# Choosing the prompt's first experts head by head, in a fused two-layer diffusion step

## The chip, the cores and the metric

The kernel runs as one program on one core of a Trainium2 chip. The metric is the device time of one execution in microseconds (us); lower is better. The engines are called PE (TensorE, matmuls), DVE (VectorE), ACT (ScalarE), POOL (GpSimd) and SP (SyncE, which here only starts transfers).

## The reference, cut to what matters

Two layers run over a prompt block of 128 tokens and a sample of 256 tokens, called P and S. Layer 0 mixes with a bidirectional mLSTM, layer 1 with attention; behind each mixer comes a layer that picks, for each token and each of 8 heads, 16 of 16384 experts. That layer is what the change is about:

```python
def one_block(xb):                                     # 128 tokens
    q = (xb @ w_q).reshape(128, P_HEADS, 2, 128)
    s = jnp.einsum('tphd,phnd->tphn', q, subkeys)      # 128 keys in each of two sets a head
    s1, i1 = lax.top_k(s[:, :, 0], 16)
    s2, i2 = lax.top_k(s[:, :, 1], 16)
    cand = (s1[..., :, None] + s2[..., None, :]).reshape(128, P_HEADS, 256)
    cidx = (i1[..., :, None] * 128 + i2[..., None, :]).reshape(128, P_HEADS, 256)
    top, pos = lax.top_k(cand, 16)
    eidx = jnp.take_along_axis(cidx, pos, axis=-1)
    g = jax.nn.softmax(top, axis=-1)
    act = gelu(jnp.einsum('tped,td->tpe', u[eidx], xb))
    return jnp.einsum('tpe,tped->td', g * act, v[eidx])
```

The prompt's mLSTM also returns its final state (`new_C`, `new_n`, `new_m`, each for two directions).

## The kernel before, in words

**Six phases of gathers.** Each pair of a layer and a token block (three blocks, two layers) is a phase of 64 groups of two expert slots. For every slot POOL starts one indirect transfer, which brings for each of 128 tokens its expert's row of u and v (8 KB): 1 MB a slot, 768 slots in all. DVE forms the dot product with u against `xrep`, the tokens copied for it; ACT makes gelu, the share and a small diagonal matrix; PE adds v times that matrix into `acc`. The rows live in a ring of 14 places (`rows`, 7 groups). From the second turn on POOL waits until the group that had the place before is summed.

**One order for all engines.** `plan()` writes the whole program as a list of steps, and each engine walks it in order (`in_order` moves a few steps on ACT and DVE). Steps named here: `NT` puts the normalised tokens transposed into `hT`; `PQ` is a quarter of the query projection (4 PSUM tiles, copied out by ACT), `PS` the scores of that quarter's two heads; `PT` the top 16 of each key set, `PC` the candidates' top 16, `PG` the experts' numbers, `PW` the shares; `MLU` is the state update of one direction (four PSUM tiles, copied out by DVE), `STATE` starts the state's transfers to memory on ACT's queue; `XR` makes `xrep` (4 PSUM tiles a half, copied by ACT); `MR` and `MC` compute a part of the modulation; `GROUPS` are groups of experts. There are six PSUM tiles, used in turn: PE can open the next only when the engine that empties it has read what stood there six tiles before.

**Where weights are put.** SP walks a list of loads of 512 KB (`weight_loads`). Before the first gathers the expert rows are free, so the first 99 loads take turns over 33 places: five of `wt` and 28 halves of `rows`. From the load after `("MR", 1, 0, 3)` on only the five places of `wt` are used. A load waits until the PSUM tile that last used its place is full (`sp.wait_ge(tile_full, free)`), and SP starts its loads in order. POOL's first 14 gathers wait in the same way for the last use of their row as a weight place.

**The opening of the first phase.** The prompt's first quarter of the choice was split in two heads already, but with one projection and one score tile. The steps stand as NT, MLU twice, STATE, PQ 0, PS 0, PQ 1, XR twice; then come the choices of head 0 and head 1. The scores and candidates lie in `sc` and `cand`, which share their memory with what the state's transfers read, so `PC` of head 0 waits for those:

```python
if s[1:] == (*FIRST_SCORES[1:], 0):

    dve.wait_ge(state_out, 96)
```

POOL's first gather waits for the first increment of `experts_chosen`, which is the end of head 0's `PG`.

Of the kernel before, what the change touches and what calls it, by code (L numbers as in the profile page):

```python
# [19 lines left out]
P = 128  # L20
# [66 lines left out]
def plan():  # L87
# [157 lines left out]
FIRST_SCORES = ("PS", 0, "P", 0, 0)  # L245
# [5 lines left out]
def in_order(who):  # L251
# [27 lines left out]
def psum_tiles(s):  # L279
# [29 lines left out]
    if k == "PQ":  # L309
        return "AAAA"  # L310
# [17 lines left out]
def weight_tiles(s, A):  # L328
# [19 lines left out]
    if k == "PQ":  # L348
        return cols(A["peer_w_q"], 8 * s[1] + 2 * s[3], 2, 2)
    if k == "PS":  # L350
        return [(A["subkeys"][QUARTERS * s[1] + s[4]], nb_of(s) - 1)]
# [3 lines left out]
EARLY = WRING + 2 * RING * GS  # L355

def weight_loads(A):
# [29 lines left out]
def needed(i, who):  # L388
# [6 lines left out]

    if s[0] in ("PT", "PC", "PG", "PW") and s[1:5] == FIRST_SCORES[1:]:
        return PLAN.index(FIRST_SCORES) + 1
# [8 lines left out]
    if s[0] == "XR":  # L406
        return after("NT") if who == "P" else PLAN.index(FIRST_SCORES)
# [47 lines left out]
def trunk(nc, A, O):  # L455
    ctx = ExitStack()
    with ctx:
# [338 lines left out]
        def _(pe):  # L796
# [48 lines left out]
            def by_feature(n_tokens):  # L845

                for j in range(2):
# [77 lines left out]
            for n_entry in in_order("P"):  # L925
# [121 lines left out]
                elif k == "PQ":  # L1047
                    by_feature(P * len(BLOCKS[s[2]]))
# [65 lines left out]
        def _(act):  # L1114
# [54 lines left out]
            for n_entry in in_order("A"):  # L1169
# [143 lines left out]
                elif k == "PQ":  # L1313
                    _, l, g, q = s
                    n = P * len(BLOCKS[g])
                    for i in range(4):
                        copy_tile(i, qTp[:, 4 * q + i, 0:n], n)
# [68 lines left out]
        def _(dve):  # L1386
# [46 lines left out]

            def weigh(s):

                _, l, g, b, part, *half = s
                blk = BLOCKS[g][b]
                nh = 1 if half else QH
                part = half[0] if half else part
                n = slice(part * nh * TOPK, (part + 1) * nh * TOPK)  # L1440
                gs, gr = (gsum[:, 2 * part:2 * part + 2], grec[:, part:part + 1]) if half else (gsum, grec)
                dve.wait_ge(top_exp, next_of(top_exp))
                V.reciprocal(gr[:, 0:nh], gs[:, nh:2 * nh]).then_inc(dve_chain, one())
                dve.wait_ge(dve_chain, noted())
                shares = topc[:, part * nh:(part + 1) * nh, :].rearrange("p c (j k) -> p k c j", k=2)
                gates = gate[:, blk, n].rearrange("p (j c t) -> p t c j", c=nh, t=2)
                for h, t, kk in QUADRANT_MOVES:
                    src, dst = quadrant(2 * h + t), quadrant(2 * h + kk)
                    last = V.tensor_tensor(gates[dst, t], shares[src, kk], bc(gr[src, 0:nh], TOPK // 2), ALU.mult)  # L1449
# [5 lines left out]
            for n_entry in in_order("D"):  # L1455
# [14 lines left out]
                if k == "GROUPS":  # L1470
                    if s[3] == 0:

                        dve.wait_ge(experts_chosen, QUARTERS * GORDER.index((s[1], s[2])) + 1 + (s[1:3] != (0, 0)))
# [199 lines left out]
                elif k == "OUT":  # L1673
# [18 lines left out]
                    last.then_inc(dve_step, 1)  # L1692
                elif k == "PS":
                    n = slice(2 * QH * s[4], 2 * QH * (s[4] + 1))
                    if s[3] == 0:
# [3 lines left out]
                elif k == "PT":  # L1699
# [3 lines left out]
                    if len(s) > 5:  # L1703
                        n = slice(2 * s[5], 2 * s[5] + 2)
                        scores = scores[:, n, :]
                    top16(top1[:, n, :], i1u[:, n, :], [scores[:, e, :] for e in range(n.stop - n.start)])
                elif k == "PC":
# [5 lines left out]
                    if s[1:] == (*FIRST_SCORES[1:], 0):  # L1713

                        dve.wait_ge(state_out, 96)
                    at = 0
                    for i0, m, w in PAIRS:
                        c4 = cand[:, 0:nh, at:at + m * w].rearrange("p h (i j) -> p h i j", j=w)
# [4 lines left out]
                    top16(topc[:, n, :], posu[:, n, :], [cand[:, h, 0:NPAIRS] for h in range(nh)])  # L1723
                elif k == "PW":
                    weigh(s)
                elif k == "PG":
# [23 lines left out]
                    place_of = [cand[:, 0:nh, :].rearrange("p a b -> p (a b)"), sc[:, 2 * part * nh:2 * (part + 1) * nh, :].rearrange("p a b -> p (a b)")]  # L1750
# [26 lines left out]
                    dve.wait_ge(dve_chain, noted())  # L1777
                    chosen = [e12[:, a, n].rearrange("p (c j k) -> p k c j", c=nh, k=2) for a in range(2)]
# [5 lines left out]
                    if not half:  # L1784
                        weigh(s)
# [161 lines left out]
```

## Time and profile before

| what | value |
|---|---|
| three timed runs | 2361.65, 2361.05, 2360.09 us; median 2361.05 |
| the profiled execution, its own time | 2359.27 us |
| its span in the profile | 2357.5 us |
| busy, share of the span | PE 67%, DVE 66%, POOL 37%, ACT 36% |
| moved | 956.48 MB, mean 406 GB/s |
| mean granted clock of PE | 0.814 |

The span runs from the first to the last instruction; the execution's own time has 1.77 us more around it. Busy shares are means over stages with different limits, so no engine's share says by itself what the kernel waits for.
### The profile page before, as it was taken

What the parts mean: (1) busy time and instruction counts of PE and PEld (TensorE: products, weight loads), DVE (VectorE), ACT (ScalarE), POOL (GpSimd) and SP (SyncE); (2) the same over time, 40 slices, a digit from 0 to 9 for tenths busy, and PEclk for the clock granted to TensorE, in tenths of its full rate; (3) what the DMA queues carried; (4) which work ended last, traced back from release to release, by engine and by line L of the source; (5) the groups of instructions that cost most, each with busy time, mean ns of one, the idle gap of its engine ahead of it and who ended that gap; (6) DMA issues with size and microseconds to landing.
All of it is one profiled execution on the core that took longest, in us unless ns stands there. A gap on an engine that the chain in (4) does not pass through costs nothing. (4 is left out here: it accounts for less than half of the span.)

```text
span 2357.5 us, 29053 instructions
## 1 busy us (share of the span) xinstructions
PE 1569.6 (67%) x9366; PEld 845.2 (36%) x9366; DVE 1567.3 (66%) x4321; ACT 844.8 (36%) x2753; POOL 867.2 (37%) x772
## 2 busy tenths in 40 slices
PE   8897977787846556556646676788766545555554
PEld 6784734565521112324321353455433102100010
DVE  2357988557677795465796567665765897665654
ACT  2324355423222333453233435443322334232232
POOL 0014334433424325243435343424434444444351
PEclk8998988898976667878967898888889777777777
DMA  9979999999999999999999999999999999999996
GB/s 387 408 269 414 373 397 415 417 418 415 416 418 420 419 419 420 417 371 419 417 420 421 418 404 420 414 381 401 418 419 420 422 420 421 422 422 421 422 422 273
DMA packets 156955, 956.48 MB, mean 406 GB/s; under 512 B 19076, under 2 KB 21764, under 8 KB 58500
## 3 DMA queue, kind: packets, MB, share of 16 engines
q0 software_dynamic: 110592, 805.36, 82.5%
q1 hardware_dynamic: 40880, 144.94, 15.6%
q10 hardware_dynamic: 5332, 4.33, 0.7%
q8 instruction: 75, 1.23, 0.2%
q14 instruction: 76, 0.62, 0.1%
HBM read 951.67 MB, written 2.89 MB: 405 GB/s over the span
## 5 line engine op out<-in xcount | busy, mean ns | idle before, releaser
L789 POOL DMA_INDIRECT rows<-in_uv,eidx x768 | 866.9, 1129 | 1449.3 <-PE acc L872 1067.1
L1429 DVE CUSTOM_DVE_ANT_0 rows<-rows,xrep 128x1024 f32<-128x1024 f32 x768 | 911.9, 1224 | 380.0 <-DMA rows<-in_uv,eidx 354.5
L872 PE MATMUL acc<-rows,diag 128*32 128x512 f32 x3072 | 745.6, 747 | 494.4 <-ACT diag L1119 463.5
L872 PEld LDWEIGHTS acc<-rows,diag 128*32 128x32 f32 x3072 | 151.9, 126 | 978.2 <-ACT diag L1119 628.8
L1119 ACT ACTIVATE act_out<-act_in 128x2 f32<-128x2 f32 x384 | 77.6, 202 | 944.4 <-DVE act_in L1429 898.4
L807 PE MATMUL bank<-wt,hT 128*128 128x256 f32 x888 | 204.0, 389 | 23.9 <-DMA wt<-in_attn_w_qkv 6.9
L1119 ACT ACT_TABLE_LOAD x123 | 157.8, 1283 | 166.4 <-DVE act_in L1429 74.3
L1119 ACT ACTIVATE diag<-small,wv 128x32 f32<-128x32 f32 x768 | 204.9, 314 | 12.5
L807 PEld LDWEIGHTS bank<-wt,hT 128*128 128x128 f32 x888 | 170.5, 194 | 62.9 <-issue 18.7
L1119 ACT ACTIVATE wv<-act_out,gate 128x1 f32<-128x1 f32 x768 | 184.3, 287 | 12.6
L807 PE MATMUL bank<-hT,wt 128*128 128x256 f32 (+1 forms) x896 | 175.0, 356 | 9.8 <-DMA wt<-in_peer_w_q 6.5
L807 PEld LDWEIGHTS bank<-hT,wt 128*128 128x128 f32 x896 | 152.5, 194 | 39.1 <-issue 9.9
L834 PE MATMUL bank<-small,arena 128*128 128x128 f32 x216 | 41.2, 352 | 103.4 <-DVE arena L1499 38.8
L1119 ACT ACTIVATE arena<-bank 128x256 f32<-128x256 f32 (+2 forms) x150 | 50.3, 376 | 164.3 <-PE bank L807 136.1
L807 PE MATMUL bank<-small,hT 128*32 128x128 f32 (+1 forms) x1584 | 75.8, 309 | 16.9 <-issue 12.5
L834 PEld LDWEIGHTS bank<-small,arena 128*128 128x128 f32 x216 | 33.5, 184 | 120.1 <-issue 115.5
L807 PEld LDWEIGHTS bank<-small,hT 128*32 128x32 f32 (+1 forms) x1584 | 62.6, 128 | 32.0 <-issue 25.1
L1429 DVE DVE_READ_ACCUMULATOR2_ANT act_in<- 128x1 f32 x768 | 63.8, 83 | 0.0
L807 PE MATMUL bank<-wt,cs 128*32 128x256 f32 x480 | 49.4, 451 | 11.1 <-DMA wt<-in_ada_w 11.0
L807 PE MATMUL bank<-arena 128*128 128x257 f32 (+3 forms) x232 | 50.9, 432 | 6.0 <-DVE arena L1647 4.4
L1686 DVE TENSOR_TENSOR arena<-bank,Nn 128x256 f32<-128x256 f32 x24 | 10.2, 424 | 66.6 <-PE bank L807 66.6
L834 PE MATMUL bank<-small,hT 128*128 128x128 f32 x112 | 24.3, 393 | 45.1 <-ACT hT L1119 35.9
(177 smaller groups left out, 1446.0 us busy)
## 6 DMA issues: line engine op xcount, KB each, us to landing
wt<-in_ada_w SPq DMA_DIRECT2D x60, 512.0 KB
wt<-in_peer_w_q SPq DMA_DIRECT2D x48, 512.0 KB
rows<-in_ada_w SPq DMA_DIRECT2D x36, 512.0 KB, 15.0
wt<-in_mlstm_w_in SPq DMA_DIRECT2D x27, 512.0 KB
rows<-in_uv,eidx POOLq DMA_INDIRECT x768
wt<-in_attn_w_qkv SPq DMA_DIRECT2D x24, 512.0 KB
rows<-in_mlstm_w_in SPq DMA_DIRECT2D x21, 512.0 KB, 15.9
rows<-in_peer_w_q SPq DMA_DIRECT2D x16, 512.0 KB, 13.7
```

The costliest lines, as they stand in the source:

```text
L789: nc.gpsimd.indirect_dma_start(out=rows[:, r, :], out_offset=None, in_=A["uv"], in_offset=bass.IndirectOffsetOnAxis(ap=eidx[:, b, slot:slo ...
L807: return nc.tensor.matmul(out, lhsT, rhs, start=start, stop=stop)
L834: last = nc.tensor.transpose(out[:, i * P:(i + 1) * P], a, ident)
L872: last = nc.tensor.matmul(acc[c:c + QUAD, h * 512:(h + 1) * 512], diag[:, r, :], rows[:, r, D + h * 512:D + (h + 1) * 512], start=first, s ...
L1119: return nc.scalar.activation(out, in_, func, **kw)
L1429: last = V.tensor_tensor_reduce(out=rows[:, r, 0:D], in0=rows[:, r, 0:D], in1=xrep[:, GS * odd + j, :], scale=1.0, scalar=0.0, op0=ALU.mul ...
L1686: V.tensor_tensor(tmp, t[:, 0:WC], gbc[:, c], ALU.mult).then_inc(dve_freed, 1)
```

## The change

Six things are changed together, all in the opening of the first phase.

1. `PQ 0` and `PS 0` are cut by heads: a projection of two PSUM tiles, then the scores of that head alone (two matmuls over 128 tokens), for head 0 and then head 1.
2. The scores of these two heads go to blocks 1 and 2 of `eidx` and their candidates to blocks 1 and 2 of `gate`, tables which the sample needs only later. The wait for the state's transfers is gone.
3. `MLU` (twice) and `STATE` stand behind `PQ 1`, and on DVE head 1's choice stands behind the copies of `MLU`.
4. The experts are dealt to slots by four quadrants of tokens, 16 moves of 32x4 in place of 8 of 32x8 for each head; POOL may begin group 0 after head 0's first 8 moves and group 1 after all 16.
5. Groups of the first 16 take the halves of `xrep` in turn (`upper`, `starts`), not the first eight the lower and the next eight the upper one.
6. The 33 early weight places are used in another order (`LAP`), which starts with `rows`.

```diff
-    yield from (("NT", 0, 1, 0), *cell(["MLU"], 0), *cell(["MLU"], 1), ("STATE",))
-    yield from (("PQ", 0, "P", 0), ("PS", 0, "P", 0, 0), ("PQ", 0, "P", 1), ("XR", 0, 0, 0), ("XR", 0, 0, 1))
-    yield from ((k, 0, "P", 0, 0, half) for half in range(2) for k in ("PT", "PC", "PG"))
-    yield from (("PW", 0, "P", 0, 0, half) for half in range(2))
+    yield ("NT", 0, 1, 0)
+    for head in range(2):
+        yield from (("PQ", 0, "P", 0, head), ("PS", 0, "P", 0, 0, head))
+    yield from (("PQ", 0, "P", 1), *cell(["MLU"], 0), *cell(["MLU"], 1), ("STATE",), ("XR", 0, 0, 0), ("XR", 0, 0, 1))
+    for head in range(2):
+        yield from ((k, 0, "P", 0, 0, head) for k in ("PT", "PC", "PG"))
+    yield ("PW", 0, "P", 0, 0)
...
-FIRST_SCORES = ("PS", 0, "P", 0, 0)
+FIRST_SCORES = [("PS", 0, "P", 0, 0, head) for head in range(2)]
...
-        for k, half in (("PW", 1), ("PW", 0), *((k, half) for half in (1, 0) for k in ("PG", "PC", "PT"))):
-            i = PLAN.index((k, *FIRST_SCORES[1:], half))
-            order.remove(i)
-            order.insert(order.index(PLAN.index(FIRST_SCORES)) + 1, i)
+        for behind, steps in ((FIRST_SCORES[0], [(k, *FIRST_SCORES[0][1:]) for k in ("PT", "PC", "PG")]),
+                              (("MLU", "P", 1, 0), [*((k, *FIRST_SCORES[1][1:]) for k in ("PT", "PC", "PG")), ("PW", 0, "P", 0, 0)])):
+            for s in reversed(steps):
+                i = PLAN.index(s)
+                order.remove(i)
+                order.insert(order.index(PLAN.index(behind)) + 1, i)
...
+LAP = [*range(WRING, WRING + 20), *range(WRING), *range(WRING + 20, EARLY)]
...
-                place = n % EARLY if i <= last_early else n % WRING
+                place = LAP[n % EARLY] if i <= last_early else n % WRING
...
+        first_sc = eidx[:, 1:3, :].bitcast(F32)
+        first_cand = gate[:, 1:3, :].rearrange("p a b -> p (a b)").unsqueeze(1)
...
-            return (0, QG // 2) if order == 0 else (0, 1)
+            return 0, 1
...
-            return g // (QG // 2) if (order, g // QG) == (0, 0) else g % 2
+            return g % 2
...
-                    if g % QG == 0 or g == QG // 2:
-                        pool.wait_ge(experts_chosen, g // QG + 1 + (g > 0))
+                    if g % QG == 0 or g in (1, QG // 2):
+                        pool.wait_ge(experts_chosen, g // QG + 1 + (g > 0) + (g > 1))
...
+                elif s in FIRST_SCORES:
+                    if s == FIRST_SCORES[0]:
+                        _, place, turn, _ = loads[used[0]]
+                        used[0] += 1
+                        first_keys = weight_place(place)
+                        pe.wait_ge(w_in[place], 16 * turn)
+                    t = open_tile(0)
+                    for a in range(2):
+                        e = 2 * s[5] + a
+                        last = mm(t[:, a * NKEYS:(a + 1) * NKEYS], qTp[:, e, 0:P], first_keys[:, e * NKEYS:(e + 1) * NKEYS], True, True)
+                    last.then_inc(tile_full, 1)
...
+                elif s in FIRST_SCORES:
+                    dve.wait_ge(tile_full, full(0))
+                    V.tensor_copy(first_sc, tile(0)[:, 0:2 * NKEYS].rearrange("p (e n) -> p e n", n=NKEYS)).then_inc(dve_freed, 1)
...
-                    if s[1:] == (*FIRST_SCORES[1:], 0):
-
-                        dve.wait_ge(state_out, 96)
+                    pairs = first_cand if len(s) > 5 else cand
...
+                    if half:
+                        chosen = [e12[:, a, n].rearrange("p (j k) -> p k j", k=QUADS) for a in range(2)]
+                        experts = eidx[:, blk, n].rearrange("p (j q) -> p q j", q=QUADS)
+                        for q in range(QUADS):
+                            for kk in range(QUADS):
+                                last = V.scalar_tensor_tensor(experts[quadrant(kk), q], chosen[0][quadrant(q), kk], 1.0 / PACK,
+                                                              chosen[1][quadrant(q), kk], ALU.mult, ALU.add)
+                            if q == QUADS - 1 or (q == 1 and half == [0]):
+                                last.then_inc(experts_chosen, 1)
+                        continue
```

The instructions of PE from the transposes of `NT` to the projection `PQ 3`, before. `arena,xrep` with 257 columns is `MLU`, `hT,rows` or `hT,wt` a projection (`x32` is a whole quarter), `rows,arena` the scores, and `small,hT` with 32 rows is `XR`.

```order
L834 MATMUL bank<-small,arena 128x128 x8
L807 MATMUL bank<-arena,xrep 128x257 x8
L807 MATMUL bank<-hT,rows 128x128 x32
L807 MATMUL bank<-rows,arena 64x128 x8
L807 MATMUL bank<-hT,rows 128x128 x32
L807 MATMUL bank<-small,hT 32x128 x128
L807 MATMUL bank<-rows,arena 64x128 x8
L807 MATMUL bank<-hT,rows 128x128 x32
L807 MATMUL bank<-rows,arena 64x128 x8
L807 MATMUL bank<-hT,rows 128x128 x32
```

The same stretch of PE in the changed kernel:

```order
L848 MATMUL bank<-small,arena 128x128 x8
L821 MATMUL bank<-hT,rows 128x128 x16
L821 MATMUL bank<-rows,arena 128x128 x2
L821 MATMUL bank<-hT,rows 128x128 x16
L821 MATMUL bank<-rows,arena 128x128 x2
L821 MATMUL bank<-hT,rows 128x128 x32
L821 MATMUL bank<-arena,xrep 128x257 x8
L821 MATMUL bank<-small,hT 32x128 x128
L821 MATMUL bank<-rows,arena 64x128 x8
L821 MATMUL bank<-hT,rows 128x128 x32
L821 MATMUL bank<-wt,arena 64x128 x8
L821 MATMUL bank<-hT,wt 128x128 x32
```

`MLU` has moved from ahead of the first projection to behind the third piece of it, directly ahead of `XR`; head 0's scores stand behind 16 matmuls in place of 40.

The instructions of DVE between the second half of `NT` (`hT`) and the choice of head 0, before:

```order
L1507 TENSOR_SCALAR hT<-bank,gain,modT 128x128 x4
L1655 COPY arena<-bank 128x257 x8
L1698 COPY arena<-bank 128x512
L1406 MAX Nn<-arena 128x8 x2
L1409 MAX_INDEX arena<-Nn,arena 128x8 x2
L1412 MATCH_REPLACE arena<-Nn,arena 128x128 x2
L1415 MAX Nn<-arena 128x8 x2
L1418 MAX_INDEX arena<-Nn,arena 128x8 x2
```

In the changed kernel the copies of `MLU` (128x257) stand here, between head 0's last step and head 1's first:

```order
L1811 SCALAR_TENSOR_TENSOR arena<-arena 128x16
L1814 TENSOR_TENSOR eidx<-eidx,Nn 128x256
L1816 TENSOR_REDUCE arena<-eidx 128x16
L1823 SCALAR_TENSOR_TENSOR eidx<-arena 32x4 x16
L1730 COPY eidx<-bank 128x256
L1690 COPY arena<-bank 128x257 x8
L1432 MAX Nn<-eidx 128x8 x2
```

The eight copies no longer stand between `NT` and head 0; the copy that empties head 1's score tile stands behind all of head 0's moves.

The loads that SP starts around the first phase's opening, before (the last row's first four loads use the `wt` places that `MR 0,4` has left):

```order
L771 DMA wt<-in_ada_w 128x1024 x5
L771 DMA rows<-in_ada_w 128x1024
L771 DMA rows<-in_peer_w_q 128x1024 x4
L771 DMA rows<-in_subkeys 128x512
L771 DMA rows<-in_peer_w_q 128x1024 x4
L771 DMA rows<-in_subkeys 128x512
L771 DMA rows<-in_peer_w_q 128x1024 x4
L771 DMA rows<-in_subkeys 128x512
L771 DMA rows<-in_peer_w_q 128x1024 x4
L771 DMA rows<-in_ada_w 128x1024 x8
L771 DMA wt<-in_subkeys 128x512
L771 DMA wt<-in_mlstm_w_in 128x1024 x24
```

And in the changed kernel:

```order
L785 DMA rows<-in_ada_w 128x1024 x8
L785 DMA rows<-in_peer_w_q 128x1024 x2
L785 DMA rows<-in_subkeys 128x512
L785 DMA rows<-in_peer_w_q 128x1024 x6
L785 DMA rows<-in_subkeys 128x512
L785 DMA rows<-in_peer_w_q 128x1024 x4
L785 DMA wt<-in_subkeys 128x512
L785 DMA wt<-in_peer_w_q 128x1024 x4
L785 DMA rows<-in_ada_w 128x1024 x8
L785 DMA wt<-in_subkeys 128x512
L785 DMA wt<-in_mlstm_w_in 128x1024 x24
```

The `wt` places now hold the keys of `PS 2` and the projection `PQ 3`, so the next keys (256 KB) and the first four loads of the sample's `mlstm_w_in` (2 MB) wait, all behind one another, for tiles of `PS 2` and `PQ 3`, the last of which is PSUM tile 120 of the program. In return rows 0 to 6 are free once `PQ 1` is done (before: rows 0 to 4); rows 7 to 9 wait for `PS 1` and `PQ 2`, rows 10 to 13 for the four `MR 1,0`, as rows 5 to 13 did before for `PQ 2`, `PS 2`, `PQ 3` and `MR 1,0`.

## Rows read from the trace of the kernel before

**Rows 1.** The page: the gathers' queue: packets, MB, share of 16 engines' time.

```profile
q0 software_dynamic: 110592, 805.36, 82.5%
```

**Rows 2.** Windows: us, busy of PE, PEld, DVE, ACT, POOL, PEclk, DMA share, GB/s.

```profile
100.00:120.00 20.00, 18.84 (x153) 15.05 (x152) 5.55 (x16) 7.32 (x19) 0.00 (x0) 1.00 1.03 408
144.00:163.00 19.00, 18.63 (x371) 17.78 (x371) 12.57 (x64) 5.57 (x12) 1.77 (x2) 1.00 0.23 23
285.00:290.00 5.00, 5.00 (x26) 2.56 (x26) 4.58 (x19) 0.00 (x0) 0.47 (x1) 1.00 0.53 178
305.00:310.00 5.00, 3.08 (x13) 1.10 (x14) 2.02 (x4) 1.55 (x7) 2.37 (x2) 1.00 0.75 216
```

**Rows 3.** Timeline from hT to the first gather: start, us, engine, line, operation.

```profile
134.56 1.50 ACT L1119 ACTIVATE hT<-bank,modT,gain 128x128 f32<-128x128 f32 x4 [1.71 <-PE bank L834]
...
138.03 7.31 PE L807 MATMUL bank<-hT,rows 128*128 128x128 f32 x64
...
145.70 1.09 PE L807 MATMUL bank<-rows,arena 128*64 128x128 f32 x16 [0.37 <-ACT arena L1119]
...
146.94 0.69 DVE L1698 COPY arena<-bank 128x512 f32<-128x512 f32 x1 [7.98 <-PE bank L807]
...
153.14 0.43 DVE L1719 TENSOR_TENSOR arena<-Nn 128x16 f32<-128x16 f32 x4 [2.35 <-DMA out_new_m<-st]
...
159.28 1.37 DVE L1782 SCALAR_TENSOR_TENSOR eidx<-arena 32x8 uint32<-32x8 f32 x8
...
160.93 1.07 POOL L789 DMA_INDIRECT rows<-in_uv,eidx  x1 [160.48 <-DVE eidx L1782]
```

**Rows 4.** Timeline: MLU on PE and DVE, first and last of ACT's six transfer issues.

```profile
134.34 3.84 PE L807 MATMUL bank<-arena,xrep 128*128 128x257 f32 x16
...
136.20 2.75 DVE L1655 COPY arena<-bank 128x257 f32<-128x257 f32 x8 [0.19 <-ACT hT L1119]
...
137.73 0.43 ACTq L1278 DMA_DIRECT2D out_new_C<-arena  x1
...
141.64 0.73 ACTq L1280 DMA_DIRECT2D out_new_m<-st  x1
```

**Rows 5.** Timeline of PE: XR, PQ 2 in pieces, PQ 3.

```profile
154.06 7.19 PE L807 MATMUL bank<-small,hT 128*32 128x128 f32 x256
...
162.21 2.66 PE L807 MATMUL bank<-hT,rows 128*128 128x128 f32 x20
...
168.14 6.09 PE L807 MATMUL bank<-hT,rows 128*128 128x128 f32 x41 [1.17 <-issue]
...
175.62 7.41 PE L807 MATMUL bank<-hT,rows 128*128 128x128 f32 x64
```

**Rows 6.** Timelines of DVE, PE and POOL: the waits up to 290 us.

```profile
194.21 0.49 DVE L1719 TENSOR_TENSOR arena<-Nn 128x32 f32<-128x32 f32 x4 [1.82 <-PE bank L807]
...
211.30 1.94 PE L834 MATMUL bank<-small,arena 128*128 128x128 f32 x8 [13.02 <-DVE arena L1499]
...
289.53 0.94 POOL L789 DMA_INDIRECT rows<-in_uv,eidx  x1 [25.90 <-PE acc L872]
```

**Rows 7.** Timeline of PE: first and last pieces of three later XR halves.

```profile
898.67 1.51 PE L807 MATMUL bank<-small,hT 128*32 128x128 f32 x48
...
904.92 3.26 PE L807 MATMUL bank<-small,hT 128*32 128x128 f32 x56 [0.45 <-issue]
...
1247.90 3.84 PE L807 MATMUL bank<-small,hT 128*32 128x128 f32 x126
...
1659.21 1.25 PE L807 MATMUL bank<-small,hT 128*32 128x128 f32 x28
...
1667.23 5.39 PE L807 MATMUL bank<-small,hT 128*32 128x128 f32 x94 [1.01 <-issue]
```

**Rows 8.** DMA queues from 140 to 142 us: packets, MB, share of 16 engines.

```profile
q10 hardware_dynamic: 540, 0.41, 63.0%
q1 hardware_dynamic: 80, 0.27, 39.6%
```

More of the change, by code:

```diff
@@ L348, in weight_tiles @@
     if k == "PQ":
-        return cols(A["peer_w_q"], 8 * s[1] + 2 * s[3], 2, 2)
+        return cols(A["peer_w_q"], 8 * s[1] + 2 * s[3] + sum(s[4:]), 1 if len(s) > 4 else 2, 2)
     if k == "PS":
+        if s in FIRST_SCORES:
+            between = sum(len(psum_tiles(t)) for t in PLAN[PLAN.index(FIRST_SCORES[0]):PLAN.index(FIRST_SCORES[1])])
+            return [(A["subkeys"][QUARTERS * s[1] + s[4]], between)] if s == FIRST_SCORES[0] else []
         return [(A["subkeys"][QUARTERS * s[1] + s[4]], nb_of(s) - 1)]
@@ L394, in after @@
         return max(j for j in range(i) if PLAN[j][0] in kinds) + 1
-    if s[0] in ("PT", "PC", "PG", "PW") and s[1:5] == FIRST_SCORES[1:]:
-        return PLAN.index(FIRST_SCORES) + 1
+    if s[0] == "PW":
+        return PLAN.index(FIRST_SCORES[1]) + 1
+    if s[0] in ("PT", "PC", "PG") and len(s) > 5:
+        return PLAN.index(FIRST_SCORES[s[5]]) + 1
     if s[0] == "MLN":
@@ L406, in needed @@
     if s[0] == "XR":
-        return after("NT") if who == "P" else PLAN.index(FIRST_SCORES)
+        return after("NT") if who == "P" else PLAN.index(FIRST_SCORES[0])
     if s[0] == "NORM" and s[3] == 2:
@@ L843, in by_token, with by_feature @@
                         product(t[:, 0:WC], lambda k: hT[:, k, tok(b)], lambda k: w(k)).then_inc(tile_full, 1)
-            def by_feature(n_tokens):
-                for j in range(2):
+            def by_feature(n_tokens, tiles=2):
+                for j in range(tiles):
                     w = weights()
@@ L1313, in _ @@
                 elif k == "PQ":
-                    _, l, g, q = s
+                    _, l, g, q, *head = s
                     n = P * len(BLOCKS[g])
-                    for i in range(4):
-                        copy_tile(i, qTp[:, 4 * q + i, 0:n], n)
+                    first = 4 * q + 2 * sum(head)
+                    for i in range(2 if head else 4):
+                        copy_tile(i, qTp[:, first + i, 0:n], n)
                 elif k == "XR":
@@ L1704, in _ @@
                         n = slice(2 * s[5], 2 * s[5] + 2)
-                        scores = scores[:, n, :]
+                        scores = first_sc
                     top16(top1[:, n, :], i1u[:, n, :], [scores[:, e, :] for e in range(n.stop - n.start)])
@@ L1722, in _ @@
                     dve.wait_ge(dve_chain, noted())
-                    top16(topc[:, n, :], posu[:, n, :], [cand[:, h, 0:NPAIRS] for h in range(nh)])
+                    top16(topc[:, n, :], posu[:, n, :], [pairs[:, h, 0:NPAIRS] for h in range(nh)])
                 elif k == "PW":
-                    weigh(s)
+                    weigh_first()
                 elif k == "PG":
@@ L1749, in _ @@
                                            cst("strides").unsqueeze(1).to_broadcast([P, nh, TOPK]), ALU.mult, ALU.add).then_inc(dve_chain, one())
-                    place_of = [cand[:, 0:nh, :].rearrange("p a b -> p (a b)"), sc[:, 2 * part * nh:2 * (part + 1) * nh, :].rearrange("p a b -> p (a b)")]
+                    spare = (first_cand, first_sc) if half else (cand[:, 0:nh, :], sc[:, 2 * part * nh:2 * (part + 1) * nh, :])
+                    place_of = [a.rearrange("p a b -> p (a b)") for a in spare]
                     V.tensor_tensor(place_of[0].rearrange("p (s e) -> p s e", e=TOPK), bc(pij[:, 0, n], TOPK),
@@ L1777, in _ @@
                     dve.wait_ge(dve_chain, noted())
+                    if half:
+                        chosen = [e12[:, a, n].rearrange("p (j k) -> p k j", k=QUADS) for a in range(2)]
+                        experts = eidx[:, blk, n].rearrange("p (j q) -> p q j", q=QUADS)
+                        for q in range(QUADS):
+                            for kk in range(QUADS):
+                                last = V.scalar_tensor_tensor(experts[quadrant(kk), q], chosen[0][quadrant(q), kk], 1.0 / PACK,
[3 more added lines that the diff above has]
+                        continue
                     chosen = [e12[:, a, n].rearrange("p (c j k) -> p k c j", c=nh, k=2) for a in range(2)]
@@ L1783, in _ @@
                     last.then_inc(experts_chosen, 1)
-                    if not half:
-                        weigh(s)
+                    weigh(s)
                 elif k == "AN":
```

33 lines of the change are left out of this document (20 added, 13 removed).

## The prediction

> **What bounds it now.** I read the page's list of DMA queues first: the gathers' queue alone takes 82.5% of the DMA engines' time [rows 1]. So the kernel is bound by bytes, except where no bytes are asked for. I looked for such places in windows of 5 us. The one at the opening is by far the largest that the change touches: from 144 to 163 us the share is 0.23 at 23 GB/s, against 1.03 at 408 GB/s before it [rows 2]. Its end is the first gather, started at 160.93 us [rows 3]. The next two holes are at 285 to 290 us (share 0.53, so 2.35 us empty) and 305 to 310 us (0.75, 1.25 us empty) [rows 2].
>
> The timeline says what ends each. The first gather waits for a chain: hT complete at 134.56 + 1.50 = 136.06; PE starts the projection at 138.03, behind MLU [rows 3, 4]; scores at 145.70; DVE copies them at 146.94, waits 2.35 us for the state's transfers until 153.14, and moves the experts' numbers from 159.28 [rows 3]. The hole at 285 us ends otherwise: POOL has waited 25.90 us for a sum by PE, until 289.53 [rows 6]. Behind that sum stands no late transfer but a chain of compute: DVE waited for PE until 194.21, PE then 13.02 us for DVE until 211.30 [rows 6]. What decides the end of that hole is therefore how early PE is through `PQ 2` and `PQ 3` (183.03 us, [rows 5]), and not when the first gather starts. From 310 us on the same bytes remain in both kernels, so the whole kernel shifts by what this chain shifts.
>
> **The change, part by part.** I time both paths from hT at 136.06.
>
> *First gather.* The projection starts about 136.2, not 138.03: 1.8 us earlier. It has two tiles of four, 7.31 / 4 = 1.83 us each: 3.7 us less [rows 3], so it ends at 139.9. The score matmuls are a quarter of 1.09 us by records (4 of 16), and the copy is half as large; from the rows of 1.09 and 0.69 us I take 1.0 us off, between 0.3 and 1.1. The wait of 2.35 us goes. The moves: 8 of 16 are needed, and DVE's 8 moves of 32x8 take 1.37 us [rows 3]; I take the smaller ones at the same 0.17 us each, so nothing is gained. Sum 1.8 + 3.7 + 1.0 + 2.3 = 8.8 us: first gather at 152.1 us. Group 1 needs 8 more moves, 1.4 us, hidden behind the two issues of group 0 (1.07 us and as much again).
>
> *What that gains in bytes.* Before, the loads ran until about 140.8 us (the queue q1 has 39.6% of 140 to 142 [rows 8]). Now the last 2.25 MB of them (one of 256 KB, four of 512 KB) must wait for tile 120; at 408 GB/s [rows 2] that is 5.5 us of transfer taken out of the quiet time and put behind the gathers. The state's 1 MB, which ran in the hole, now runs among the gathers: at least 2.6 us by its bytes; its queue showed 63% of 2 us for 0.41 MB [rows 8], so up to 3.2 us for 1.05 MB by that row. So of 8.8 us some 8.1 to 8.7 us are given back. On the bytes alone the change is worth 0 to 0.7 us. A small new hole comes too: ten rows are free before `PQ 3` is done, 10 x 2.6 us (1.05 MB each at 408 GB/s), so they and the state last from about 154 until 183 us, and the next work comes 2 us behind tile 120. The holes at 285 and 305 us have 3.6 us of slack for this, so the bytes do not decide.
>
> *PE's chain.* Head 0's projection and scores end at 140.6, head 1's (3.7 + 0.4 + the 0.37 us wait for ACT) at 145.1, `PQ 1` (7.31) at 152.4. Then MLU: its second tile needs the PSUM tile of head 1's scores, and DVE empties that only behind head 0's 16 moves: 152.1 - 0.3 + 1.4 + 0.35 = 153.6. Seven tiles of 3.84 / 8 = 0.48 us [rows 4] follow: 157.0. XR thus starts 3.0 us later than its 154.06 [rows 5]. Queued behind the last MLU copy are ACT's six issues, 137.73 to 142.37 = 4.64 us [rows 4], so ACT copies XR's first tile only at 162; PE needs that tile back for its seventh, at 157.0 + 6 x 0.9 = 162.4, so this costs 0.2 us. Unhindered, XR (7.19 us) ends at 164.4, and score, `PQ 2`, score, `PQ 3` take 1.0 + 7.4 + 1.4 + 7.4 = 17.2: 181.6 us, 1.4 us *earlier* than 183.03.
>
> But before, `PQ 2` was not unhindered: it took from 162.21 to 168.14 + 6.09 = 174.23, 12.0 us against 7.4 for the same 64 records in `PQ 3`, in pieces, the last behind a gap of 1.17 us that ends in "issue" (no releaser in the profile), right after the gathers began [rows 5]. XR, with four times the instructions per us, had run just before it without a gap, in the empty DMA. Now XR itself runs under gathers. Later halves of XR do so: 898.67 to 908.18 is 9.5 us and 1659.21 to 1672.62 is 13.4 us, for 128 records that took 3.6 us in the first; yet the one at 1247.90 took 3.84 for 126 [rows 7]. So the loss around XR is between 0.5 us (two halves like 1247.90) and 15.7 us (5.9 + 9.8). I take the nearest row, the 4.6 us that `PQ 2` lost in this very stretch: 186.2 us, or **3.2 us later** than before.
>
> The Trainium skill (Runtime: NRT & Kernel Launch, "Instruction fetch mechanics") says that fetch crosses a 16 KiB boundary at the cost of one tail bump, "mostly hidden". By that rule the loss would be nothing and the chain 1.4 us earlier; the gaps of rows 5 and 7 speak against it where gathers fill the queues.
>
> *DVE's chain.* Head 1 starts 157.4 + 0.1 instead of 160.68, and takes as long plus 1.4 us for its extra moves; the shares wait for ACT, which is busy with XR's copies and then 2 exponentials. It is 1 us early to 1 us late at the first dot product, and then waits for PE's `PS 2` either way. Part 5 costs nothing, since both halves of `xrep` are there before the first dot product; nor do the first 66 loads of part 6, each of which waits for the same tile as before. The cover of the shares' lateness is PE's delay; without it they would cost up to 1 us.
>
> **The sum.** Against the profiled execution: 2359.27 + 3.2 = 2362.5 us. The median of the timed runs is 1.78 us above that execution, so I predict 2364.3 us, +0.14%. A measurement of this kernel tells some 0.2% (4.7 us) from no change.
>
> **The rivals.**
> - *Instruction supply under gathers costs PE more.* From 6.1 us of loss on (4.7 + 1.4) the kernel is slower by over 0.2%. At the mean of the three halves of rows 7 (5.9, 0.3 and 9.8: 5.3 us each) the two halves lose 10.6 us, the shift is +9.2, and the time 2370.3 us. For it: two of the three halves. Against: the third, and that the stretch of rows 5 itself lost 4.6 us in all.
> - *No loss.* PE's part in the sum is -1.4 us: 2359.7 us. For it: the row at 1247.90. Against: the gaps in rows 5 came with the first gathers.
> - *The early gather passes through.* If the stretch to 290 us is bound by the gathers after all, the 8.8 us count, less what the bytes give back: 2352.3 us if the deferred loads find another hole, 2360.4 if not. For it: 82.5% of all DMA time is gathers. Against: POOL's 25.90 us wait for PE.
>
> **Chances.** The forecast (loss of 2 to 6 us) 0.41; more loss 0.33; no loss 0.13; the early gather passes 0.13, of which 0.11 below the 0.2% line. So faster 0.11, same 0.56 (0.41 + 0.13 + 0.02), slower 0.33. The range 2355 to 2371 us leaves out most of the early-gather case and the worst fetch losses.
>
> **What the changed profile would show.** First gather at 152 us: the top part is right. DMA empty from about 135.5, not 141, to 154 us: the deferred loads are. PE idle near 153 us for a DVE copy of eidx; XR starting near 157 and broken by gaps that end in "issue"; `PQ 3` ending near 186 us; POOL's long wait ending near 293 and not 289.5 us. `PQ 3` before 183 us would make the prediction wrong on the low side, after 189 on the high side. If POOL's wait ends earlier although `PQ 3` is later, the chain I followed was not the one that binds.

## The result, and the profile after

The changed kernel takes 2373.14 us (median of 6 runs, 2370.18 to 2374.8) beside 2361.35 us for the kernel before, run on the same chip (median of 6, 2359.56 to 2366.41): a ratio of 1.0044, 95% interval 1.0031 to 1.0057. It is slower by 10.4 us by the ratio, 11.8 between the medians; the forecast was +3.2. The profiled execution took 2370.18 us.

The diff ahead of the prediction leaves out one line, and the text there says that the wait for the state's transfers is gone. It has moved: DVE now waits for `state_out` 96 ahead of its copy of the scores of `PS 2`. In the changed kernel PE's scores come later than the transfers (row at 187.19 below), so the omission does not bear on the sum; in one experiment this wait binds.

The timeline of the changed kernel (start, us, engine, line, operation), from hT to the end of the wait that stood at 289.53 us in [rows 6]. ACTq and SPq are these engines' transfer issues.

```profile
134.77 1.50 ACT L1144 ACTIVATE hT<-bank,modT,gain 128x128 f32<-128x128 f32 x4 [1.71 <-PE bank L848]
...
136.33 3.84 PE L821 MATMUL bank<-hT,rows 128*128 128x128 f32 x32 [1.61 <-ACT hT L1144]
...
152.64 1.07 POOL L803 DMA_INDIRECT rows<-in_uv,eidx  x1 [152.19 <-DVE eidx L1823]
...
156.41 0.43 ACTq L1303 DMA_DIRECT2D out_new_C<-arena  x1
156.88 0.57 ACTq L1304 DMA_DIRECT2D out_new_n<-arena  x1
...
157.51 5.22 PE L821 MATMUL bank<-small,hT 128*32 128x128 f32 x181
...
158.80 10.98 ACTq L1304 DMA_DIRECT2D out_new_n<-arena  x1
...
165.27 0.63 PE L821 MATMUL bank<-small,hT 128*32 128x128 f32 x11 [2.54 <-issue]
...
169.81 2.09 ACTq L1305 DMA_DIRECT2D out_new_m<-st  x1
172.17 3.54 ACT L1144 ACTIVATE xrep<-bank 128x512 f32<-128x512 f32 x7 [18.81 <-issue]
...
172.82 3.64 PE L821 MATMUL bank<-small,hT 128*32 128x128 f32 x64 [6.92 <-ACT xrep L1144]
...
178.53 0.94 POOL L803 DMA_INDIRECT rows<-in_uv,eidx  x1 [17.37 <-PE bank L821]
...
186.98 7.41 PE L821 MATMUL bank<-hT,wt 128*128 128x128 f32 x64
...
187.19 0.69 DVE L1739 COPY arena<-bank 128x512 f32<-128x512 f32 x1 [1.75 <-PE bank L821]
...
194.79 3.10 SPq L785 DMA_DIRECT2D wt<-in_mlstm_w_in  x4
...
298.85 0.94 POOL L803 DMA_INDIRECT rows<-in_uv,eidx  x1 [23.63 <-PE acc L886]
```

Up to 157.51 us this is the forecast: first gather 152.64 (152.1 was forecast), XR from 157.51 (157.0). Then ACT's issue of the second `new_n`, whose twin took 0.57 us just before, takes 10.98 us, and `new_m` behind it 2.09. ACT copies nothing from 156.41 to 172.17; PE waits 6.92 us for a PSUM tile. Having stood still, PE goes on at the lower of its two clocks (granted 0.50 from 170 to 175 us, below): its next 64 records take 3.64 us, where 64 of the 256 in [rows 5] take 1.80. `PQ 3` ends at 186.98 + 7.41 = 194.39 us, 11.4 us behind the 183.03 of [rows 5]. Its PSUM tiles release the 100th load and those behind it on SP (194.79). POOL, out of free rows after seven gathers, waits 17.37 us. And its long wait ends at 298.85 us, 9.3 us behind [rows 6].

The windows of the changed kernel (us, busy of PE, PEld, DVE, ACT, POOL, PEclk, DMA share, GB/s):

```profile
135.00:140.00 5.00, 3.67 (x32) 3.65 (x32) 1.23 (x4) 1.55 (x5) 0.00 (x0) 1.00 0.01 4
155.00:160.00 5.00, 5.00 (x104) 4.38 (x107) 4.72 (x18) 0.00 (x0) 3.74 (x4) 1.00 0.93 349
170.00:175.00 5.00, 2.18 (x44) 2.03 (x48) 0.00 (x0) 2.83 (x6) 0.00 (x0) 0.50 1.02 404
175.00:180.00 5.00, 5.00 (x60) 4.34 (x53) 0.67 (x5) 3.28 (x8) 0.94 (x1) 0.70 0.84 79
180.00:185.00 5.00, 5.00 (x48) 5.00 (x47) 4.78 (x17) 0.83 (x3) 0.93 (x1) 1.00 1.10 168
190.00:195.00 5.00, 5.00 (x54) 4.62 (x56) 4.93 (x23) 0.83 (x3) 0.00 (x0) 1.00 0.56 236
```

The hole of [rows 2] now runs from 135 to 152 us, and a second one has opened at 175 to 200 us. There the share hides it in part: at 175 to 180 us the engines are busy 0.84 of the time and move 79 GB/s. The queues of that stretch say with what (packets, MB, share of 16 engines' time); the first fence is of 175 to 180 us, the second of 155 to 195 us, the third of the kernel before from 136 to 160 us.

```profile
q10 hardware_dynamic: 772, 0.35, 81.9%
q0 software_dynamic: 10, 0.04, 2.0%
```

```profile
q0 software_dynamic: 1423, 10.35, 73.5%
q10 hardware_dynamic: 2116, 1.05, 17.5%
```

```profile
q10 hardware_dynamic: 2116, 1.05, 31.8%
q1 hardware_dynamic: 492, 1.76, 20.1%
```

The state's 1.05 MB are 2116 packets. They took 17.5% of 40 us, so 7.0 us of all 16 engines, and before 31.8% of 24 us, 7.6 us, in a time that was free. The prediction had 2.6 to 3.2 us, by bytes and by a look at 2 us of them ([rows 8]), which happened to hold mostly large packets. But not all of the 7.0 us were taken from the gathers: by 175 us, when the gathers ran out, this queue had used 11.0, 14.6 and 13.8% of three stretches of 5 us, 2.0 us in all. The other 5 us fell into the second hole, 4.1 of them from 175 to 180 us.

To see where time was lost I added up the bytes in windows of 5 us and noted when each kernel had moved so much (us behind the kernel before):

```
MB moved     60     65     70     85    110    150    600    700    950
after       0.6   11.8   14.0   13.5    9.9   13.4   14.4    8.8    9.0
```

At 60 MB, about 171 us, the changed kernel is level: the first gathers came 8.3 us earlier, and the loads not made before were the price. Then 11 to 13 us go within 10 MB. Between 85 and 116 MB, where the kernel before has its holes at 285 and 305 us, the lag falls to 8.1 us (5.4 come back, 3.6 were forecast), but a hole at 325 us (share 0.34), which the kernel before has not, takes them again. 5.6 us come back between 600 and 700 MB.

### The profile page after: what moved, and what is told of

Its sections match the earlier page's. It is cut to its first block and busy times, and to the rows that moved or that the text cites. A ratio compares the mean times of both kernels' runs of the same rounds, so it can differ in the third digit from the quotient of the medians.

```text
span 2368.4 us, 29062 instructions
## 1 busy us (share of the span) xinstructions
PE 1566.3 (66%) x9358; PEld 833.7 (35%) x9358; DVE 1571.5 (66%) x4337; ACT 845.3 (36%) x2753; POOL 868.3 (37%) x772
## 3 DMA queue, kind: packets, MB, share of 16 engines
q1 hardware_dynamic: 40880, 144.94, 15.5%
## 5 line engine op out<-in xcount | busy, mean ns | idle before, releaser
L886 PE MATMUL acc<-rows,diag 128*32 128x512 f32 x3072 | 763.2, 758 | 502.0 <-ACT diag L1144 494.1
L821 PE MATMUL bank<-hT,wt 128*128 128x256 f32 (+1 forms) x1024 | 189.7, 347 | 7.4 <-DMA wt<-in_peer_w_q 4.6
L821 PEld LDWEIGHTS bank<-hT,wt 128*128 128x128 f32 x1024 | 167.6, 195 | 37.3 <-issue 9.4
L821 PE MATMUL bank<-small,hT 128*32 128x128 f32 (+1 forms) x1584 | 63.0, 289 | 18.5 <-ACT xrep L1144 8.7
L821 PEld LDWEIGHTS bank<-small,hT 128*32 128x32 f32 (+1 forms) x1584 | 55.8, 120 | 27.4 <-issue 9.8
L821 PE MATMUL bank<-wt,cs 128*32 128x256 f32 x408 | 42.6, 448 | 8.4 <-DMA wt<-in_ada_w 8.4
## 6 DMA issues: line engine op xcount, KB each, us to landing
rows<-in_ada_w SPq DMA_DIRECT2D x45, 512.0 KB, 13.8
```

The source lines that it names most:

```text
L821: return nc.tensor.matmul(out, lhsT, rhs, start=start, stop=stop)
L886: last = nc.tensor.matmul(acc[c:c + QUAD, h * 512:(h + 1) * 512], diag[:, r, :], rows[:, r, D + h * 512:D + (h + 1) * 512], start=first, s ...
```

## Three theories before the experiments

The letters are those of the recorded expectations. *Held issues (A).* ACT, held 15.5 us in the six issues, makes PE and then POOL and the loads late. *Instruction supply (B)*, the rival from the prediction: gathers slow PE's instructions through XR. *Bytes and places (C).* The state's packets and the later loads run among the gathers; with the turned places the 100th load waits for PSUM tile 120, and the DMA engines have too little to do until `PQ 3` is done. The kernels of a group ran on one chip beside the kernel before, whose median was 2363.13 us for the first four, 2359.39 for the next four and 2362.69 for the last two. Single executions of one kernel differ by 5 to 16 us, so what one profile shows is compared by its waits, and times by medians and ratios.

## Experiments: each part undone alone

**The state's transfers on SP's queue**, ahead of the 100th load.

```diff
-    act.dma_start(O["new_C"] ...)   # new_n, new_m alike, in STATE
+    sp.dma_start(O["new_C"] ...)    # SP's list of loads, ahead of load 99
```

> The changed kernel, but SP starts the six transfers of the state (it stands idle there, waiting for PSUM tile 120) and ACT none. Theory A (ACT is held in the issue of the state's transfers, 156.41 to 171.90 us in the changed kernel, and PE waits 6.92 us for its copies of XR): the wait for XR's copies is gone, PQ 3 ends between 183 and 187 us in place of 194.4, and the time falls by 6 to 10 us, to 2363 to 2367. Theory B (instruction supply under gathers, the gap of 2.54 us and what hides behind ACT): XR still takes over 15 us and the time falls by less than 4 us. Theory C (bytes: the later loads and the state's transfers among the gathers): no change, 2371 to 2375, since all bytes go at the same time as before.

2378.84 us, ratio 1.0068 (1.0046 to 1.0091). The hold went along to SP (timeline of this kernel):

```profile
158.53 11.78 SPq L789 DMA_DIRECT2D out_new_n<-arena  x1
```

So the hold belongs to the transfer, not to ACT. PE was through `PQ 3` at 180.76 + 7.41 = 188.17, 6.2 us sooner than in the changed kernel, and the time rose nevertheless, for the wait that the change had moved now ended last (timeline of DVE):

```profile
191.68 0.69 DVE L1742 COPY arena<-bank 128x512 f32<-128x512 f32 x1 [11.74 <-DMA out_new_m<-st]
```

DVE's sums came later, and PE waited for DVE until 223.39 us, which in [rows 6] ended at 211.30. The 2363 to 2367 us of theory A did not come; with this other wait in the way, the run does not test what a free ACT is worth.

**Without the two transfers of `new_n`** (that output is left out).

```diff
-    act.dma_start(O["new_n"] ...)
-    sent["state_out"] += 3
+    sent["state_out"] += 2
...
-    dve.wait_ge(state_out, 96)
+    dve.wait_ge(state_out, 64)
```

> The changed kernel without the two transfers of new_n (512 elements of 4 bytes each; that output is left out). Theory A, with the small elements as the reason that an issue is held: ACT is through with the other four issues within 3 us, and the time falls by 6 to 10 us. If any transfer is held that is issued while gathers fill the queues, new_C is held instead and the time falls by less than 3 us. Theory B: falls by less than 4 us. Theory C: the state's queue had most of its packets from new_n, so it falls by 2 to 4 us.

2371.02 us, ratio 1.0032 (1.0018 to 1.0045). ACT's four issues took 161.28 to 163.79, none held: no issue is held without `new_n` and its 4-byte pieces. But the time fell by only 2 us. In this execution hT came 3.5 us later than in [rows 3] (138.02); XR then stood between gaps without a releaser, one row of which is shown from PE's timeline, and `PQ 3` was done at 193.09: 6.6 us behind the kernel before, if the late start is taken off.

```profile
166.16 0.27 PE L821 MATMUL bank<-small,hT 128*32 128x128 f32 x1 [1.15 <-issue]
```

**MLU and STATE back ahead of the first projection**, the rest of the change left in. (On DVE, head 1's choice stands directly behind head 1's scores again.)

```diff
-    yield ("NT", 0, 1, 0)
+    yield from (("NT", 0, 1, 0), *cell(["MLU"], 0), *cell(["MLU"], 1), ("STATE",))
...
-    yield from (("PQ", 0, "P", 1), *cell(["MLU"], 0), *cell(["MLU"], 1), ("STATE",), ("XR", 0, 0, 0), ("XR", 0, 0, 1))
+    yield from (("PQ", 0, "P", 1), ("XR", 0, 0, 0), ("XR", 0, 0, 1))
```

> The changed kernel with MLU and STATE back ahead of the first projection, as before the change; the projection by heads, the score tables, the 16 moves and the turned places stay. First gather at 154 to 155 us (two later than in the changed kernel). Theory A: the state's issues take 4.6 us again, in the empty DMA, and the time is 2359 to 2365. Theory B: XR now begins near 154.5 us with the gathers, as slow as in the changed kernel without ACT's part: 2364 to 2368. Theory C: the state's bytes are back in the quiet time (3 us), the loads are not: 2368 to 2371.

2371.42 us, ratio 1.0038 (1.0024 to 1.0052). The issues fall into the empty DMA again, the first gather comes at 155.13, `PQ 3` ends at 189.10, and again the time falls by 2 us at most. The share of DMA at 185 to 190 us is 0.14: there the loads and rows behind `PQ 3` are missing.

**The weight places turned back**, the rest left in.

```diff
-LAP = [*range(WRING, WRING + 20), *range(WRING), *range(WRING + 20, EARLY)]
+LAP = [*range(EARLY)]
```

> The changed kernel with the early weight places in the old order, so that the 2.25 MB of loads behind MR 1,0 start at 132 us again and rows 5 to 9 are free later. Theory C: 5.5 us of transfers are back in the quiet time, the time falls by 4 to 6 us. Theories A and B: PE's chain is not touched, so within 2 us of the changed kernel.

2372.8 us, ratio 1.0041 (1.0026 to 1.0055): nothing gained. ACT was held again, and `PQ 3` ended at 194.94, in an execution in which hT came 2.8 us later than in the changed kernel's (137.58). Only five rows were free at first, and POOL waited 19.51 us for the sixth.

```profile
163.40 9.31 ACTq L1304 DMA_DIRECT2D out_new_n<-arena  x1
```

By the ratios the four gave -0.24, 0.12, 0.06 and 0.03% of 0.44. A single cause among them would have shown itself here, unless a new wait hid it, as in the first. Either each of A and C hides the other, or the cause is another. The next runs undid two things together, and put B to the test.

## Experiments: two together, and the instruction supply

**MLU back and places turned back.** The two diffs above together.

> a3_mlu_back with the early weight places in the old order as well: what is left of the change is the projection by heads, the score tables, the moves and the first gather at about 155 us. In a3 PQ 3 ended 6 us later than in the kernel before, and the bytes moved by 220 us lagged by 8.6 us. If the later 2.25 MB of loads make the difference between the two (theory C as a part), the lag falls to about 3 to 5 us and the time is 2364 to 2367. If PE's chain alone sets the time (theories A and B), nothing changes against a3, 2369 to 2372. If the early first gather is worth what the shorter path to it says (6 us), 2357 to 2360.

2360.97 us, ratio 1.0009 (0.9997 to 1.002): level with the kernel before. Against the run with MLU back alone, the places are worth 0.29% by the ratios, some 7 us. XR had one gap, in the timeline of PE:

```profile
157.82 5.22 PE L821 MATMUL bank<-small,hT 128*32 128x128 f32 x181
164.50 2.37 PE L821 MATMUL bank<-small,hT 128*32 128x128 f32 x75 [1.46 <-issue]
...
176.63 7.41 PE L821 MATMUL bank<-hT,rows 128*128 128x128 f32 x64
```

**First gather held until XR is done** (all else as changed).

```diff
+            pool.wait_ge(tile_full, 110)
             for n, (l, b) in enumerate(GORDER):
```

> The changed kernel with one more wait: POOL starts its first gather only when XR's last PSUM tile is full (tile 110), near 165 us in place of 152.6. XR and the issues of the state's transfers then run in the empty DMA. Theories A and B (the early gathers hold ACT and PE up): ACT's issues take 4.6 us, XR 7.2 to 7.7 us, PQ 3 ends at 182 to 188 us in place of 194.4, and the time is the changed kernel's or up to 6 us less although the gathers start 12 us later. Theory C (bytes): the empty stretch is 12 us longer, and the time rises by 6 to 12 us, to 2379 or more.

2380.59 us, ratio 1.0094 (1.008 to 1.0109). This tells three things. ACT's issues took 156.80 to 161.97 us, 5.2 us: the hold comes with the gathers. The first gather came at 174.31, 21.7 us later than in the changed kernel, and the kernel is 7.5 us slower between medians, 12 us by the ratios. That is less than the 21.7 us, but it is a net figure, as ACT was free here and `PQ 3` ended at 191.19 us, 3.2 us sooner. And XR, with no gather in flight, had these gaps (timeline of PE):

```profile
157.90 4.05 PE L822 MATMUL bank<-small,hT 128*32 128x128 f32 x129
164.40 0.27 PE L822 MATMUL bank<-small,hT 128*32 128x128 f32 x1 [2.44 <-issue]
165.56 1.20 PE L822 MATMUL bank<-small,hT 128*32 128x128 f32 x4 [0.90 <-issue]
169.12 4.90 PE L822 MATMUL bank<-small,hT 128*32 128x128 f32 x122 [2.36 <-issue]
```

So B, as the prediction put it, falls: the gaps need no gathers. The DMA engines were not idle, though. From 160 to 165 and from 165 to 170 us the state's packets alone kept them at shares of 1.26 and 0.92, with 65 and 40 GB/s.

**XR right behind head 0's scores**, with MLU back.

```diff
+    yield from (("PQ", 0, "P", 0, 0), ("PS", 0, "P", 0, 0, 0), ("XR", 0, 0, 0), ("XR", 0, 0, 1))
+    yield from (("PQ", 0, "P", 0, 1), ("PS", 0, "P", 0, 0, 1), ("PQ", 0, "P", 1))
```

> a3_mlu_back with XR (which needs hT only) moved ahead, directly behind head 0's scores, where PE's work has 12 us before the gathers start; head 1's projection and scores and PQ 1 follow. Theory B (instruction supply under gathers costs XR 6 to 9 us): XR takes 7.2 to 7.7 us, PE's chain gains 5 to 9 us against a3, PQ 3 ends at 181 to 185 us, and the time falls to 2362 to 2366. If PE's projections lose the same time in place of XR: PQ 3 ends at 187 to 190 us, 2368 to 2371. Theory C alone: no change against a3, since the bytes start at the same times.

2367.51 us, ratio 1.0038 (1.0023 to 1.0052). XR ran from 143.94 and still had gaps of 3.38 and 2.34 us, before any gather (first one 157.07). The first gap, from 146.33 us, fell among the state's packets; in the second, from 154.75 to 157.09 us, no DMA packet of any kind started. So the second gap had no traffic beside it. `PQ 3` ended at 191.38 us, not at the 181 to 185 that were expected of a quick XR.

**The same with the places turned back.**

> b3_xr_ahead with the early weight places in the old order. Rows 1 to 6 are free later than in b3 (with head 1's scores, PQ 1 and PQ 2), the 2.25 MB of loads start at 132 us again. If both PE's chain and the bytes count, this is the best of the four, 2357 to 2362, level with the kernel before or up to 4 us below it. If the later rows cost what the loads give back: as b3.

2361.48 us, ratio 1.0001 (0.9987 to 1.0015), although one gap of XR alone was 5.41 us in the profiled execution (itself 2367.78 us). Again the places are worth 6.0 us, here within one group.

**The kernel before, with the places turned alone.**

```diff
-                place = n % EARLY if i <= last_early else n % WRING
+                place = LAP[n % EARLY] if i <= last_early else n % WRING
```

> The kernel before with nothing changed but the order of the weight places. Theory (the turned places cost by themselves: 2.25 MB of loads behind PSUM tile 120 add to the DMA-idle time around 160 to 200 us): the pairs that differ in the places alone, with MLU ahead of the first projection, gave 10.5 and 6.0 us, so 2367 to 2371 us, ratio 1.0025 to 1.0045; loads stop near 135.5 us and not at 141, and the bytes between 65 and 85 MB are moved 5 us later. Rival A (the places cost only together with the early gather, which leaves no other bytes to move until PQ 3): the gathers start at 161 as before and fill the queues until their rows run out, so the total stays within 0.1% of the kernel before. Rival B (the places help here, since rows 0 to 6 are free for gathers earlier): faster by 0.1 to 0.2%.

2366.12 us (12 runs), ratio 1.0015 (1.0005 to 1.0025): 3.4 us, between the theory and rival A of this expectation. One wait was unforeseen. Without loads beside it the state's transfer ended no sooner but later, and head 0 waited for it (timeline of DVE, then the queues from 145 to 150 us: 0.04 MB in a share of over 1):

```profile
156.64 0.43 DVE L1720 TENSOR_TENSOR arena<-Nn 128x16 f32<-128x16 f32 x4 [5.40 <-DMA out_new_m<-st]
```

```profile
q10 hardware_dynamic: 274, 0.04, 119.4%
```

So 3.5 us of late first gather (164.42) are in that run's time, and it is no clean measure of the places.

**The changed kernel without `new_n` and with the places turned back.** MLU stays behind the third projection.

> The changed kernel with the old weight places and without the two transfers of new_n (that output is left out), MLU still behind the third projection. Each of the two alone gave almost nothing (2371.0 and 2372.8 against 2373.1 us). Theory (two limits near each other, ACT held by the issues and the loads behind tile 120, so that either alone hides the other): together they give 6 to 10 us, 2361 to 2366 us, ratio 1.000 to 1.002, PQ 3 ends 5 to 6 us after the time of the kernel before (about 188 to 189 us) and the lag in bytes at 70 MB is under 6 us. Rival (the place of MLU costs by itself, through PE's order): the time stays at 2370 to 2372 us though neither ACT nor the loads are held.

2363.48 us (12 runs), ratio 1.0007 (0.9997 to 1.0017). Alone the two gave 0.12 and 0.03%; together they give 0.37%, 8.7 us by the ratios, or 9.7 us between the medians of two groups. It is the theory's range, and the rival (the place of MLU costs by itself) falls. The issues are short, PE waits for no copy, `PQ 3` is done at 184.31, and the first gather came at 152.14:

```profile
156.38 0.62 ACTq L1304 DMA_DIRECT2D out_new_m<-st  x1
...
158.69 1.80 ACT L1144 ACTIVATE xrep<-bank 128x512 f32<-128x512 f32 x3 [5.84 <-PE bank L821]
...
164.76 2.38 PE L821 MATMUL bank<-small,hT 128*32 128x128 f32 x75 [2.54 <-issue]
...
176.90 7.41 PE L821 MATMUL bank<-hT,rows 128*128 128x128 f32 x64
```

The lags behind the kernel before, worked out as above, put it together:

```
MB moved                        58     60     65     70     85    150    950
after                          0.7    0.6   11.8   14.0   13.5   13.4    9.0
MLU back                              0.5    3.6    9.0    8.5    9.2    6.5
places back                           -0.8   11.7   13.1   12.6   15.0   15.3
MLU and places back           -4.6   -4.3   -0.2    0.9    0.5    2.6   -1.0
no new_n, places back         -5.7   -5.7    0.1    1.6    1.2    2.3   -0.8
```

With the old places and ACT free (the last two rows) the early gather does put the kernel 4.3 and 5.7 us ahead at 60 MB, and 5 MB later nothing of it is left. Only five rows are free there, and POOL waited 9.75 and 14.03 us for the sixth, which depends on `PQ 2`.

## Why the prediction was wrong, step by step

- *First gather 152.1 us*: right (152.64), as were XR's start (3.0 us later forecast, 3.45 measured), the empty DMA from 135 us on, and DVE's copy. *What that gains in bytes*: right up to 60 MB, "0 to 0.7 us" against 0.6 us behind.
- *"Queued behind the last MLU copy are ACT's six issues, 137.73 to 142.37 = 4.64 us ... so this costs 0.2 us"*: **this step failed.** The rows were of issues into a quiet DMA, and the change moves them among the gathers. They took 15.5 us and PE waited 6.92. XR ended at 172.82 + 3.64 = 176.46 us, 12.1 behind the unhindered 164.4: 0.5 by its start, 2.5 by a gap, 6.9 by this wait, and 2.3 because its records took longer, 1.8 of that in the last 64, at the granted clock of 0.50 that followed PE's standstill. ACT's copies did not set that pace: seven were done by 175.71 us, and for the eighth ACT waited 0.82 us for PE. The forecast's own 17.2 us from there give 193.7 for the end of `PQ 3`; measured 194.39, as the scores of `PS 1` took 1.85 us at the lower clock in place of 1.09. The sum had no term for the clock; it cost 2.6 of the 11.4 us, as a consequence of the wait.
- *"at least 2.6 us by its bytes ... up to 3.2 us"*: too small for the queue's whole time, 7.0 us, but of that only 2.0 us stood beside the gathers up to 175 us. That this term made the kernel slower is not shown.
- *"Ten rows are free before PQ 3 is done ... so the bytes do not decide"*: **failed too.** Seven rows were free at first, gathered by 175 us; the eighth to tenth depended on PE, which ACT held (178.53, 182.29 and 185.86 us). And tile 120, which the loads wait for, came at 194 us, where the sum had it at 186. From 175 to 195 us the DMA engines moved 79, 168, 247 and 236 GB/s in stretches of 5 us, against some 408. Turning the places back gives 0.25 to 0.37% (6 to 9 us) in three pairs of kernels in which ACT is not held, and 0.03% where it is.
- *Loss through instruction supply, 4.6 us*: only 2.6 us of the row that it was taken from are gaps (0.38, 1.06 and 1.17); in the rest PE ran slower, at a granted clock of 0.65 from 167 to 169 and 0.50 from 169 to 171 us in the kernel before. Measured were gaps of 2.54 us in the changed kernel and 1.46 to 6.4 us in all in others, and the stated reason, gathers, was wrong. The rival built on it gave 2370.3 us, near the result for another reason: of the 11.4 us only 2.5 are such a gap.
- *"What decides the end of that hole is ... how early PE is through `PQ 2` and `PQ 3`"*: borne out in the changed kernel. `PQ 3` late by 11.4 us, POOL's wait by 9.3, all bytes by 9.0. It is not the whole rule: with the transfers on SP's queue `PQ 3` was only 5.1 us late and the bytes 13.9, as DVE's wait ended last.

Shown by the runs: removing the held issues and the late loads together restores the time, and neither does alone. How the 10 us divide has no answer while each hides the other. Nor do the runs part the hold from the small packets themselves: each way of freeing ACT that brought the time back also took `new_n` out from among the gathers. For the hold speaks PE's wait of 6.92 us for ACT in the timeline. The 5.6 us that come back between 600 and 700 MB come back in every kernel (2.9 to 7.9 us): the profiled execution of the kernel before has a hole at 1575 us (share 0.31) there, which the changed kernel has not. Why is open. No kernel here beat the one before; the one with MLU and places turned back starts its gathers 4.8 us earlier (156.16) and is level with it.

## What to carry to other kernels

An issue that is moved has to be priced for the traffic that it will meet, and a transfer by its packets: read its queue over its whole life, not its bytes, and ask how much of that falls beside other work. Where a start is moved forward, count what it may use until the next release (here seven rows, 18 us), and ask what frees the eighth; gains before that point are a loan. When an engine has stood still, look at its clock before its slow pace is put down to a neighbour. When undoing parts one by one gives nothing, undo them in pairs before a cause is given up.

## What was not expected of the hardware

**Small packets beside a saturated queue.** The state's packets ran from about 160 to 183 us in the changed kernel, up to 175 us beside gathers. From 160 to 165 us the queues read

```profile
q0 software_dynamic: 243, 1.73, 86.8%
q10 hardware_dynamic: 189, 0.19, 11.0%
```

and in the next 5 us 251 packets of q0 against 253 of q10: about packet for packet, whatever their sizes; from 170 to 175 us it was 258 against 582. An issue was held at the second `new_n` in the three kernels that sent it beside gathers (10.98, 11.78 and 9.31 us), and in none without `new_n` or without gathers. The Trainium skill (DMA: Bandwidth & Descriptors, "Queues, rings and completion order") says that each DMA engine goes round the queue rows that have work, one whole packet from each, and that a packet may hold several pieces; the counts up to 170 us agree with one for one, those after it not unless the profile counts pieces. The same page ("Rules for kernel authors") says that a non-contiguous last dimension gives one descriptor per element, which agrees with the 1056 packets fewer in the kernels without `new_n` (1060 against 2116), whose elements number 1024. What fills up while the issue is held, no run shows.

**PE's instruction supply.** XR issues some 35 records a microsecond (256 in 7.19 us, [rows 5]) and stood still for up to 5.41 us at a time in the changed kernel and nine edited ones: beside gathers, beside the state's packets alone, and once with no packet in flight. In the kernel before and in the one with only the places turned it ran through with 0.58 us lost at most; both ran it after the state's packets and before the gathers' bytes, at DMA shares under 0.05. A block of instructions is a DMA packet of its own; from 162 to 164 us of the changed kernel, in the gap of 2.54 us, there is one (queue, packets, MB, share):

```profile
q8 instruction: 1, 0.02, 3.0%
```

The Trainium skill (Runtime: NRT & Kernel Launch, "Instruction fetch mechanics") calls the crossing of a block boundary "mostly hidden". If the gaps are such crossings they were not hidden here, though the kernel before passed blocks inside XR without a gap. What decides that is open, and that the gaps are the supply is not shown either: from 146 to 150 us, around the gap of 3.38 us, no instruction packet moved.
